# Weight remainders cut into eight pieces at the attention starts, and value units converted over 1120 columns

## The reference: what is computed

```
def reference(...):
    x = first_block(x, ...)        # 2 layers
    return second_block(x, ...)    # 1 layer

# first_block, each layer
h = rms_norm(x, g_pre_mix[l])
q_nsa, kv_nsa, g_nsa, qkv_sb, g_merge = split(h @ w_in)     # rope on q and k
o_nsa = nsa_attention(...)              # compressed + selected + windowed softmax, gated
o_sb = stick_breaking_attention(...)    # exp(log_sigmoid(z) + later), z causal
m = (g_a * (o_nsa @ w_proj_nsa) + g_b * (o_sb @ w_proj_sb)) @ w_out
x = x + rms_norm(m); x = x + rms_norm(conv_ffn(rms_norm(x)))

# second_block
x = x + 0.5 * rms_norm(swiglu(rms_norm(x)))
ya = neighbourhood_attention(qa, ka, va) @ w_branch_a
yb = dilated_mixture(qb, kb, vb) @ w_branch_b
x = x + rms_norm((sigmoid(gate_a) * ya + sigmoid(gate_b) * yb) @ w_out)
x = x + 0.5 * rms_norm(swiglu(rms_norm(x)))
```

## Time and profile before

| what | value |
|---|---|
| median of the runs | 2925.21 us (3 runs, 2924.9 to 2925.76) |
| span of the profiled execution, first to last instruction | 2926.2 us |
| PE busy | 2831.4 us, 97% of the span |
| DVE, ACT, POOL busy | 1231.3, 1302.1, 1168.2 us (42%, 44%, 40%) |
| mean granted TensorE clock | 0.989 |
| transfers | 249.91 MB, 85 GB/s over the span |

### The profile page before, as it was taken

How to read it: one execution, slowest core, us unless ns; L and a number is a source line. 1 busy time by engine, 2 the same in 40 slices (tenths; PEclk the granted TensorE clock), 3 DMA queues, 4 the chain that set the end, 5 groups by cost and what they waited for, 6 DMA issues and landing times.

```text
span 2926.2 us, 43251 instructions
## 1 busy us (share of the span) xinstructions
PE 2831.4 (97%) x15918; PEld 2340.0 (80%) x15918; DVE 1231.3 (42%) x2141; ACT 1302.1 (44%) x1999; POOL 1168.2 (40%) x368
## 2 busy tenths in 40 slices
PE   7999999999999999999999999999998999999999
PEld 6765688888888765788888879998896678889987
DVE  7164212555222364114555067770204531277731
ACT  5356434554335356335545254452415353444442
POOL 3300355444454100554444454454531325544453
PEclk9999999999999899999999999999999999999999
DMA  6200133233224100332332323323330213323332
GB/s 171 83 12 12 54 100 114 87 100 100 101 87 118 51 12 12 86 116 86 100 94 96 100 88 101 103 101 112 107 94 16 76 35 101 120 73 101 103 111 79
DMA packets 326468, 249.91 MB, mean 85 GB/s; under 512 B 36727, under 2 KB 294471, under 8 KB 326343
## 3 DMA queue, kind: packets, MB, share of 16 engines
q1 hardware_dynamic: 323864, 246.85, 27.2%
q10 hardware_dynamic: 2478, 1.39, 0.2%
HBM read 245.74 MB, written 2.70 MB: 85 GB/s over the span
## 4 chain that ended last, share of the span: by engine, by line
PE 80%; issue 6%; ACT 5%; DVE 4%; DVEq 2%; POOL 2%; ACTq 1%; DMA 0%; SPq 0%; POOLq 0%
PE pair L1863 62%; PE pair L2229 8%; PE pair L2071 2%; PE pair L2107 1%; PE pair L2090 1%; POOL wlo L553 1%; DVE wlo L1542 1%; PE pair L2153 1%; PE pair L2151 1%; PE pair L2139 1%; PE pair L2169 1%; ACT tmp L655 1%; ACT whi L921 0%; DVEq L1528 0%; ACT bP L1033 0%
## 5 line engine op out<-in xcount | busy, mean ns | idle before, releaser
L553 POOL TENSOR_TENSOR wlo<-raw,whi 128x2048 fp32r<-128x2048 f32 x195 | 906.8, 4650 | 1505.9 <-ACT whi L619 1505.9
L1863 PE MATMUL pair<-hh,whi 128*128 128x512 f32 x1600 | 630.2, 394 | 9.2 <-DVE hl L1183 7.2
L1863 PE MATMUL pair<-hl,whi 128*128 128x512 f32 x1600 | 626.3, 391 | 0.0
L1863 PE MATMUL pair<-hh,wlo 128*128 128x512 f32 x1600 | 626.0, 391 | 0.0
L619 ACT ACTIVATE whi<-raw 128x2048 fp32r<-128x2048 f32 x195 | 373.0, 1913 | 562.2 <-PE pair L1863 550.3
L1863 PEld LDWEIGHTS pair<-hh,whi 128*128 128x128 f32 x1600 | 302.7, 189 | 76.8 <-issue 12.4
L1863 PEld LDWEIGHTS pair<-hh,wlo 128*128 128x128 f32 x1600 | 302.5, 189 | 63.7
L1863 PEld LDWEIGHTS pair<-hl,whi 128*128 128x128 f32 x1600 | 302.6, 189 | 61.3
L2229 PE MATMUL pair<-hh,whi 128*128 128x256 f32 x640 | 185.0, 289 | 8.1 <-POOL wlo L584 6.1
L1191 DVE SCALAR_TENSOR_TENSOR pair<-pair,gp_d 128x512 f32<-128x512 f32 x32 | 22.3, 698 | 388.6 <-ACT sq L627 388.3
L2229 PE MATMUL pair<-hl,whi 128*128 128x256 f32 x640 | 181.2, 283 | 0.0
(11 more groups left out here) (350 smaller groups left out, 5314.6 us busy)
## 6 DMA issues: line engine op xcount, KB each, us to landing
raw<-in_w_in SPq DMA_DIRECT2D x118, 512.0 KB, 3.8
raw<-in_w_up SPq DMA_DIRECT2D x88, 512.0 KB, 4.2
raw<-in_ffn_w_gate SPq DMA_DIRECT2D x44, 512.0 KB, 4.0
raw<-in_ffn_w_up SPq DMA_DIRECT2D x44, 512.0 KB, 4.3
raw<-in_w_down SPq DMA_DIRECT2D x40, 512.0 KB, 3.9
raw<-in_ffn_w_down SPq DMA_DIRECT2D x40, 512.0 KB, 3.9
raw<-in_w_out SPq DMA_DIRECT2D x24, 512.0 KB, 4.1
raw<-in_w_proj_nsa SPq DMA_DIRECT2D x16, 256.0 KB, 3.8
```

What stands on the lines that cost most here:

```text
L553: pool.tensor_tensor(wlo[:, s, :], raw[:, s, :], whi[:, s, :].bitcast(f32), ALU.subtract).then_inc(lo_ready, 1)
L1863: o = pe.matmul(out, l, r, start=start and first, stop=stop and last)
```

## The change

POOL's remainder of units 11, 12 and 13 of each layer of the first block, and of units 44 and 50 of the second, is made by eight instructions of 256 columns instead of one of 2048; the first waits for ACT's copy, the last counts in `lo_ready`. That is eight remainders in all. For the four value units, ACT's copy and POOL's remainder cover columns 0 to 1119 (`VN`) instead of 2048. To place these, the loops that make remainders are cut at those units.

```diff
+VN = 4 * VG
+PIECE = 256
             def rest(v, s):
                 pool.wait_ge(hi_ready, 2 * v + s + 1)
                 pool.tensor_tensor(wlo[:, s, :], raw[:, s, :], whi[:, s, :].bitcast(f32), ALU.subtract).then_inc(lo_ready, 1)
+            def rest_in_pieces(u):
+                v, s = u // 2, u % 2
+                pool.wait_ge(hi_ready, u + 1)
+                for c in range(0, 2048, PIECE):
+                    o = pool.tensor_tensor(wlo[:, s, c:c + PIECE], raw[:, s, c:c + PIECE], whi[:, s, c:c + PIECE].bitcast(f32), ALU.subtract)
+                o.then_inc(lo_ready, 1)
+            def valued_rest(u):
+                s = u % 2
+                pool.wait_ge(hi_ready, u + 1)
+                pool.tensor_tensor(wlo[:, s, 0:VN], raw[:, s, 0:VN], whi[:, s, 0:VN].bitcast(f32), ALU.subtract).then_inc(lo_ready, 1)
+            def layer_rest(u0, first, end):
+                rest_of(first, u0 + 4)
+                valued_rest(u0 + 4)
+                valued_rest(u0 + 5)
+                rest_of(u0 + 6, u0 + 11)
+                for u in range(u0 + 11, u0 + 14):
+                    rest_in_pieces(u)
+                rest_of(u0 + 14, end)
...
-            rest_of(1, firsts[1] + 1)
+            layer_rest(0, 1, firsts[1] + 1)
...
-                rest_of(first, end)
+                if m == 2:
+                    layer_rest(UL, first, end)
+                elif m == 5:
+                    u2 = DEPTH * UL
+                    rest_of(first, u2 + 44)
+                    rest_in_pieces(u2 + 44)
+                    rest_of(u2 + 45, u2 + 50)
+                    rest_in_pieces(u2 + 50)
+                    rest_of(u2 + 51, end)
+                else:
+                    rest_of(first, end)
...
+            def valued_upper(v, s):
+                act.wait_ge(w_loaded[s], 32 * (v + 1))
+                act.wait_ge(tile_done, 4 * v + 2 * s - 2)
+                act.activation(whi[:, s, 0:VN], raw[:, s, 0:VN], ACT.Copy).then_inc(hi_ready, 1)
...
-                upper(v0 + 2, 0)
+                valued_upper(v0 + 2, 0)
                 for mt in range(2):
                     turned(v0 + 1, 1, mt, 1.0)
-                upper(v0 + 2, 1)
+                valued_upper(v0 + 2, 1)
```

More of the change, by code:

```diff
@@ L560, in rest_of @@
             def rest_of(first, end):
-                if first % 2:
+                if first % 2 and first < end:
                     rest(first // 2, 1)
```

## The result

The changed kernel takes 2898.09 us (median of 4 runs, 2895.58 to 2900.6) beside 2925.49 us of the kernel before (4 runs, 2924.9 to 2930.3): 27.4 us less, a ratio of 0.9906 with a 95% interval of 0.9892 to 0.9921. The profiled execution has a span of 2893.6 us and a mean granted clock of 0.994; it is the quickest of the four.

What follows compares the result with a forecast made beforehand. PE, busy 97% of the span, was taken as the bound, so only its waits and low clock could yield time. Terms 4.6 + 1.6 + 8.0 + 7.8 + 5.6 + 1.4 - 1.0 = 28.0 gave 2897 us, range 2888 to 2911.

Steps and rivals of the forecast that it cites:

- Value units, 4.6: PE's wait for the second value unit's remainder, both layers: shorter copy and remainder gain 2.3 us a layer.
- The cap that DVE's `kT` might go first: Value units: DVE's `kT` may precede POOL's earlier start, limiting the gain to 1.9 us a layer.
- The low clock behind the second layer's wait: Second layer's value units: 3.20 us of half-speed matmuls should go, gaining 1.6 us; nothing at the low end.
- First attention's start, 8.0: First turn, both layers: scalings end between pieces and the clock may hold, 4.0 us a layer (1.7 to 4.8).
- Third turn, 7.8: First attention's third turn, both layers: wait goes whole and clock should hold, 3.9 us a layer (2.3 to 4.1).
- A little for later pairs that meet a piece: Third turn: small deduction from 4.09 to 3.9 us a layer for later scaling pairs meeting a piece.
- Dilated and neighbourhood start, 5.6: Second block's attention starts: scalings wait for pieces only, gaining 3.7 us at the dilated and 1.9 at the neighbourhood.
- The clock behind those two, 1.4: Dilated and neighbourhood starts: clock held likely low behind the waits, up to 3.35 us each, 0.7 each counted.
- Losses, 1.0: POOL's unit 13 ends later, into the next step's sums: 0 to 1.4 us a layer, taken 0.5.
- The first rival: Attention starts and third turn: waits shrink but the clock falls all the same, 17.3 us gained, 2908; chance 0.23.
- The second, that eight pieces hold the port like one: Attentions: DVE waits until the eighth piece ends, 3.3 us slower in all, 2928; chance 0.09.
- The third, dear pieces: Attentions: port held and pieces costly, slower from 0.80 us a piece, 2954 at 1.28; chance 0.05.

Runs made afterwards that it cites:

- the paced version: The changed kernel with unit 13 whole and each piece of units 11, 12, 44, 50 waiting for one more DVE scaling: 2890.21 us, later 2888.43.
- the filled waits: The kernel before, with 10 and 8 extra PE matmuls in its waits at the first attention's start and third turn: 2918.15 us, ratio 0.9973.

## Why the prediction was right, point by point

The forecast of 2897 stands 1.1 us from the median, its sum of 28.0 beside 27.4. The mechanism is the one that was forecast: DVE gets in between the pieces, and at the first attention's start and in the third turn the clock holds. That the sum comes so near is in part luck. Single terms were off by up to 2.1 us a kernel, to both sides, and the runs of the change alone lie 5.0 us apart. Its last step, from the profiled span to the median (1.0 lower), mixes two measures, since a run's time is 2.0 us above its own span; it cost nothing here, as 28.0 from the median of before gives 2897.5. By its own terms:

- **Value units, 4.6.** Each wait fell from 2.93 to 0.21, 2.72 instead of the 2.3 taken. ACT's copy took the 1.14 that was estimated. The cap that DVE's `kT` might go first did not come: POOL began at 71.47, and `kT` at 71.63 was the one that was late (2.99 instead of 0.69). The low clock behind the second layer's wait went (1.6); the first layer's wait had none behind it before.
- **First attention's start, 8.0.** 5.09 and 5.05 a layer, over the upper bound of 4.8. The step that mis-sized it took the quiet turn's 25.46 as what an unhindered first turn needs; the paced version shows 25.03. So the loss was 5.5 a layer, and by the filled waits 3.1 of it was the clock and 2.4 the wait. And the wait that was left, 0.80, cost 0.4 beside the paced version, where about 1.0 was taken off.
- **Third turn, 7.8.** 3.40 and 3.35 a layer instead of 3.9. The pair that the earlier trace rows show no longer costs PE anything, as forecast. "A little for later pairs that meet a piece" was too little: the next step's pair, at 207.75, met two pieces and cost PE 0.50.
- **Dilated and neighbourhood start, 5.6.** The first waits shrank by 3.77 and 1.95, as taken (3.7 and 1.9). The neighbourhood's second pair of scalings was not counted; it met pieces as well and cost PE 1.17. Together 4.6 (9.3 to 5.5 and 5.3 to 4.5).
- **The clock behind those two, 1.4.** Not shown. At the dilated start the low stretch is as long after the change (2180.20 to 2187.00 at 0.50) as before (2212.30 to 2219.00). Of the wait of 1.40 there, 1.28 stays without any piece beside the scaling, and with pieces of 512, as in the second profile of the paced version, the clock had fallen before that wait began (there 0.50 from 2183.10 to 2184.30, the wait of 0.86 after it). So the scaling's wait is not what this stretch hangs on. At the neighbourhood start the clock is low from 2303.00 to 2306.40 (0.51) in the first profile of the change, but from 2300.50 to 2307.10 (0.50) in its second, as long as before.
- **Losses, 1.0.** 0.8: two waits for `oslo` of 0.9 instead of 0.5.

The first rival, that the clock falls all the same (2908), is refuted at the first start and the third turn by the windows at 1.00, and holds at the dilated start and, in part, at the neighbourhood's. The second, that eight pieces hold the port like one, is refuted by the first start: with POOL busy from 137.25 to 142.99, the two scalings end within 1.01 us of 139.13. The third, dear pieces, falls with a piece at 0.73. By the Trainium skill's GPSIMD Engine Reference, § 2.1 Instruction dispatch, GpSimd's cores go on to the next instruction without a barrier; that did not keep DVE out here. The Trainium skill's SBUF — State Buffer, § Who interferes with whom, says that whoever issues first has the shared pair of ports for the whole instruction while the other is blocked; for DVE's side the trace agrees, piece by piece, with the waits of 2.77 to 0.55 above.

What the prediction didn't foresee is the rest of the clock: about 15 us between the two profiles against some 10 in the sum. The profile of before has low windows at places where the change moves nothing, such as 126.70 to 133.50; the profile after, where the same work stands 7 us earlier, has none there:

```profile
126.70:133.50 6.80, 6.80 (x29) 5.77 (x28) 3.63 (x4) 0.87 (x2) 3.43 (x1) 0.50 0.32 88
```

```profile
118.00:132.00 14.00, 14.00 (x107) 12.07 (x106) 7.13 (x9) 4.82 (x4) 4.56 (x1) 1.00 0.31 92
```

The second profile of the paced version has one there again (124.70 to 131.50 at 0.50). Since the change's own two profiles differ in the same way, these are no effect of the change that can be counted on; the medians, which average over them, come out at the sum. What decides where the clock falls in such places stays open.

## What to carry to other kernels

Where one engine's instruction holds up another's, as POOL's does DVE's here, look at how long a single instruction holds it, not at how busy the engine is: the same work in shorter instructions, even with a quarter more of POOL's time for it, took PE's waits for `nP` from 11.6 us to 4.0 and those for `bP` from 9.3 to 5.5. If the order is fixed by hand, go a step further and place the pieces behind the instructions that they would hold up. Count every later instruction that can meet a piece, not only the one in the trace that is late now. And price a wait of a few microseconds on PE with the slower matmuls that may follow it, here 3.1 us behind a wait of 2.77 and 1.4 behind one of 2.33; a wait of 2.57 elsewhere had none behind it, so this part is a chance and not a certainty.

## What was not expected of the hardware

- A second scaling right behind the first waits for a whole further piece. In the change the first runs from 139.13 in 0.34 us, as long as one takes in the paced version, POOL's piece starts at 139.30, and the second scaling, issued at 139.39, takes 0.75:

```profile
139.13 0.34 DVE L1450 TENSOR_SCALAR nP<-nP,nstat,gate 128x128 f32<-128x128 f32 x1
...
139.30 0.76 POOL L562 TENSOR_TENSOR wlo<-raw,whi 128x256 fp32r<-128x256 f32 x1
...
139.39 0.75 DVE L1450 TENSOR_SCALAR nP<-nP,nstat,gate 128x128 f32<-128x128 f32 x1
```

  Here the two engines take turns, one instruction each, so of a pair that falls into a run of pieces the second loses most of a piece.
- Identical instruction streams have low clocks at different places in two executions. The paced version's profiles differ by 9.4 us of span (2883.1 and 2892.5) at mean clocks of 0.997 and 0.992, with turns equal to 0.01 us. In the window 97.40 to 100.80 the clock is 1.00 in the first and 0.51 in the second.
- Sixteen pieces of 128 columns cost 6.80 us at the first start, 0.43 each, less than the 0.47 that the line through the rows of 512 and 2048 columns gives.
